# A 512-token transformer block pair on Trainium2: the memory-key norms move from the differential-attention stage into the mix-output stage, and the last retention norm moves back by a tile

## What is computed

```python
def hybrid_mixer(h, w_in, ret_norm, diff_q_norm, diff_k_norm, ..., diff_norm, w_out, lam_init):
    ...
    ro = group_norm(retention(rq, rk, rv), ret_norm)      # 4 heads of 128
    ro = jax.nn.silu(rg) * ro
    dq = rms_norm(dq, diff_q_norm)                        # 4 heads of 2 x 64
    dk = rms_norm(dk, diff_k_norm)
    do = diff_attention(dq, dk, dvv, lam)                 # softmax 0 less lam times softmax 1
    do = rms_norm(do, diff_norm) * (1.0 - lam_init)       # 4 heads of 128
    return jnp.concatenate([ro, do], axis=-1) @ w_out     # "mix_out", added to x

def memory_attention(h, mem_n, w_q, w_kv, w_o, q_norm, k_norm):
    q = rms_norm(h @ w_q, q_norm)
    k = rms_norm(mem_n @ w_k, k_norm)                     # 256 memory rows, 4 heads of 256
    ...
```

## Time and profile before

| what | value |
|---|---|
| median of three executions | 2153.44 us |
| the profiled execution's own time | 2153.9 us |
| its span in the trace | 2152.1 us |
| TensorE busy | 2098.6 us, 98% of the span |
| GpSimd busy | 1387.0 us, 64% |
| VectorE busy | 752.6 us, 35% |
| ScalarE busy | 509.4 us, 24% |
| mean granted clock of TensorE | 0.993 of full speed |

### The profile page before, as it was taken

The page is one execution under the profiler, slowest core; times in us unless marked ns, Lnnn a source line. Parts: engine busy times, 40 slices in busy tenths (PEclk is TensorE's granted clock), DMA queues, the critical chain, the costliest instruction groups (busy, mean ns, idle before and its releaser), DMA issues.

```text
span 2152.1 us, 28985 instructions
## 1 busy us (share of the span) xinstructions
PE 2098.6 (98%) x9198; PEld 1671.6 (78%) x9198; DVE 752.6 (35%) x1230; ACT 509.4 (24%) x923; POOL 1387.0 (64%) x1372
## 2 busy tenths in 40 slices
PE   7999999999999999999999999999899999999997
PEld 5878866678888888878888887877667778888885
DVE  4123345434320122352223136344765452221024
ACT  2023234331210121241111012144652322110011
POOL 5743333367776777667777779655667457777675
PEclk8999999999999999999999999999999999999998
DMA  7311111123223323222233334222222112223221
GB/s 247 114 60 40 49 50 49 50 72 97 95 98 97 98 97 107 88 91 95 97 97 98 95 98 168 88 69 74 84 88 92 56 63 93 97 97 98 97 96 61
DMA packets 55683, 193.85 MB, mean 90 GB/s; under 512 B 6303, under 2 KB 8607, under 8 KB 55236
## 3 DMA queue, kind: packets, MB, share of 16 engines
q1 hardware_dynamic: 51500, 184.05, 26.1%
q10 hardware_dynamic: 4120, 8.95, 1.3%
HBM read 190.85 MB, written 5.27 MB: 91 GB/s over the span
## 4 chain that ended last, share of the span: by engine, by line
PE 92%; DVE 4%; ACT 2%; issue 1%; DMA 0%; DVEq 0%; SPq 0%; ACTq 0%
PE acc L270 26%; PE acc L272 26%; PE acc L271 26%; PE st L316 2%; PE ob L648 1%; PE sc L633 1%; PE ob L461 1%; PE sc L474 1%; PE sc L1499 1%; PE sc L476 1%; PE acc L860 1%; PE acc L859 1%; PE tp L641 1%; PE acc L858 1%; PE st L596 1%
## 5 line engine op out<-in xcount | busy, mean ns | idle before, releaser
L1704 POOL TENSOR_TENSOR w_lo<-w_raw,w_hi 128x512 fp32r<-128x512 f32 x684 | 923.3, 1350 | 57.1
L1702 POOL TENSOR_SCALAR w_hi<-w_raw 128x512 fp32r<-128x512 f32 x684 | 466.0, 681 | 688.5 <-PE acc L272 645.4
L270 PE MATMUL acc<-h_hi,w_hi 128*128 128x512 f32 x1872 | 753.3, 402 | 13.9 <-DVE h_lo L1837 8.7
L272 PE MATMUL acc<-h_hi,w_lo 128*128 128x512 f32 x1872 | 731.4, 391 | 0.0
L271 PE MATMUL acc<-h_lo,w_hi 128*128 128x512 f32 x1872 | 730.9, 390 | 0.0
L270 PEld LDWEIGHTS acc<-h_hi,w_hi 128*128 128x128 f32 x1872 | 353.4, 189 | 102.0 <-issue 24.1
L271 PEld LDWEIGHTS acc<-h_lo,w_hi 128*128 128x128 f32 x1872 | 353.4, 189 | 82.3 <-issue 10.4
L272 PEld LDWEIGHTS acc<-h_hi,w_lo 128*128 128x128 f32 x1872 | 352.8, 188 | 74.5
L270 PE MATMUL acc<-hid_hi,w_hi 128*128 128x512 f32 x608 | 236.9, 390 | 0.0
L271 PE MATMUL acc<-hid_lo,w_hi 128*128 128x512 f32 x608 | 236.5, 389 | 0.0
L272 PE MATMUL acc<-hid_hi,w_lo 128*128 128x512 f32 x608 | 236.5, 389 | 0.0
(11 more groups left out here) (253 smaller groups left out, 1905.4 us busy)
## 6 DMA issues: line engine op xcount, KB each, us to landing
w_raw<-in_wstream SPq DMA_DIRECT2D x342, 512.0 KB, 3.5
x<-in_xT SPq DMA_DIRECT2D x4, 512.0 KB, 6.7
bias_skew<-bias_rows ACTq DMA_DIRECT2D x4, 512.0 KB, 7.6
out_y<-x SPq DMA_DIRECT2D x8, 256.0 KB, 2.2
arena<-bias_skew ACTq DMA_DIRECT2D x4, 257.5 KB, 3.6
bias_skew<-bias_rows ACTq DMA_DIRECT2D x4, 256.0 KB, 7.6
arena<-in_memT ACTq DMA_DIRECT2D x1, 1024.0 KB, 7.2
arena<-in_decay ACTq DMA_DIRECT2D x1, 1024.0 KB, 11.9
```

The source lines that it names most:

```text
L270: nc.tensor.matmul(dst, w_hi[:, slot, k, :], xh[:, k, :], start=first, stop=False)
L272: done = nc.tensor.matmul(dst, w_lo[:, slot, k, :], xh[:, k, :], start=False, stop=last)
L1702: nc.gpsimd.tensor_scalar(w_hi[:, slot, ks, :], w_raw[:, raw, ks, :], 1.0, 0.0, ALU.mult, ALU.add).then_inc(w_rounded, 1)
L1704: nc.gpsimd.tensor_tensor(w_lo[:, slot, ks, :], w_raw[:, raw, ks, :], w_hi[:, slot, ks, :].bitcast(F32), ALU.subtract).then_inc(w_split, 1)
```

## The change

The stats of the memory keys leave the attention stage. Their four squares are made at once on ACT at the start of the mix-output stage, into `pt_2`; PE runs `stat_pe` of `mk0` to `mk3` after units 2, 3, 4 and 5 of the mix output; ACT runs the stat's four steps after the squares of the same block; DVE runs L340 and L347 of `mk{n-3}` after the addition of block n, and the scaling of the keys at the end of block n, for n from 3 to 6. In the attention stage the stats now lie in tiles 4 (`dq3`), 5 (`do0`), 8 (`dk3`), 9 (`do1`), 13 (`do2`); the scaling of `do` follows its stat in the same tile on DVE, its square is made in the tile of the copy out of PSUM on ACT, and the low part stays in the head's last tile. The last retention norm (`gn3`) runs on DVE in tile 0 after the copy of the first `mem_k` unit, its ACT part in tile 0 after the exponentials, its high part in tile 1 and its low part in tile 2; since the gate in slot 31 lives longer, a probability buffer moves from slot 31 to slot 30. In the mix output ACT writes the scaled block to PSUM (`tp`), copies it to the high part from there, and writes the square to PSUM (`sc`); DVE's low part and running sum read PSUM with one SBUF operand each.

```diff
-DIFF_STAT = {2: "dq3", 3: "dk3", 4: "mk0", 5: "mk1", 6: "do0", 8: "mk2", 9: "mk3", 10: "do1", 14: "do2"}
-STATS += [DIFF_STAT[_t] for _t in sorted(DIFF_STAT)] + ["do3"]
+DIFF_STAT = {4: "dq3", 5: "do0", 8: "dk3", 9: "do1", 13: "do2"}
+STATS += [DIFF_STAT[_t] for _t in sorted(DIFF_STAT)] + ["do3"] + [f"mk{_h}" for _h in range(4)]
...
-        p_d = [[a2(28), a2(29)], [a2(32), a2(31)]]
+        p_d = [[a2(28), a2(29)], [a2(32), a2(30)]]
...
         def diff_act(act):
...
+                if tile == 0:
+                    stat_act(act, "gn3", hr[:], 128)
                 if tile in DIFF_STAT:
                     stat_of(tile)
                 if h and qt == 0:
                     o_copy(h - 1)
+                    o_sq(h - 1)
...
                 copy_pt(h, qt)
-                if tile + 1 in DIFF_STAT and DIFF_STAT[tile + 1][:2] == "mk":
-                    k_sq(int(DIFF_STAT[tile + 1][2]))
-                if h and qt == 1:
-                    o_sq(h - 1)
-                if h and qt == 3:
+                if tile == 1:
+                    ret_high_act(act, 3)
+                if h and qt == 2:
                     high(h - 1)
...
         def diff_dve(dve):
...
-                if tile == 0:
-                    ret_low_dve(dve, 3)
                 if tile < 8:
                     dve.wait_ge(w_used, 2 * (U0["mem_k"] + tile + 1))
                     nc.vector.tensor_copy(mem_k[:, tile, :], acc[tile % 2][:, 0:MEM]).then_inc(acc_read, 1)
+                if tile == 0:
+                    ret_norm_dve(dve, 3)
+                if tile == 2:
+                    ret_low_dve(dve, 3)
                 if tile in DIFF_STAT:
                     name, j = DIFF_STAT[tile], int(DIFF_STAT[tile][2])
-                    if name[:2] == "mk":
-                        k_norm(j)
-                    elif name[:2] == "do":
+                    if name[:2] == "do":
                         stat_v_dve(dve, name, 128)
+                        o_norm(j)
...
         def mix_out_pe(pe):
...
                 out1(pe, "mix_out", n, n % 2, h2_hi, h2_lo)
+                if 2 <= n < 6:
+                    h = n - 2
+                    stat_pe(pe, f"mk{h}", [pt_2[:, h, 0:MEM], pt_2[:, h, MEM:2 * MEM]], [(s("mk_sq"), h + 1)], width=MEM)

         def mix_out_act(act):
+            g, b0, s0 = GAINS["norm_mem_q_2"], blocks0("mix_out"), sums0("mix_out")
+            for h in range(4):
+                nc.scalar.activation(pt_2[:, h, :].rearrange("p (b t) -> p b t", b=2), mem_k[:, 2 * h:2 * h + 2, :],
+                                     ACT.Square).then_inc(s("mk_sq"), 1)
             for n in range(8):
-                split_act(act, "mix_out", n, n % 2, h1_hi, "norm_mem_q_2", (acc_read, G0["mix_out"] + n + 1))
+                act.wait_ge(acc_read, G0["mix_out"] + n + 1)
+                act.wait_ge(h_lo, b0 + n - 1)
+                nc.scalar.activation(tp[n % 2], x[:, n, :], ACT.Identity, scale=gain[:, g + n:g + n + 1]).then_inc(s("mo_xg"), 1)
+                act.wait_ge(s("mo_xg"), n + 1)
+                nc.scalar.copy(h1_hi[:, n, :], tp[n % 2]).then_inc(h_hi, 1)
+                act.wait_ge(h_sum, s0 + n)
+                nc.scalar.activation(sc[n % 2], x[:, n, :], ACT.Square).then_inc(h_sq, 1)
+                if 2 <= n < 6:
+                    stat_act(act, f"mk{n - 2}", hr[:, 0:MEM], 256, width=MEM)

         def mix_out_dve(dve):
...
                 nc.vector.tensor_tensor(x[:, n, :], acc[n % 2], x[:, n, :], ALU.add).then_inc(acc_read, 1)
-                split_dve(dve, "mix_out", n, n % 2, h1_hi, h1_lo, "norm_mem_q_2")
+                if 3 <= n < 7:
+                    h = n - 3
+                    stat_dve(dve, f"mk{h}", hr[:, 0:MEM], 256, MEM)
+                dve.wait_ge(h_hi, b0 + n + 1)
+                nc.vector.tensor_tensor(h1_lo[:, n, :], tp[n % 2], h1_hi[:, n, :].bitcast(F32), ALU.subtract).then_inc(h_lo, 1)
+                dve.wait_ge(h_sq, b0 + n + 1)
+                dve.wait_ge(h_sum, s0 + n + 1)
+                nc.vector.tensor_tensor(ssum[:], sc[n % 2], ssum[:], ALU.add).then_inc(h_sum, 1)
+                if 3 <= n < 7:
+                    for c in range(2):
+                        z = mem_k[:, 2 * h + c, :]
+                        nc.vector.scalar_tensor_tensor(z, z, g_col("mk", c), hr[:, 0:MEM], ALU.mult, ALU.mult).then_inc(s("mk_done"), 1)
+                    dve.wait_ge(s("mk_done"), 2 * h + 2)
+                    dve.sem_inc(hr_used, 1)
```

More of the change, by code:

```diff
@@ L1096, in ret_high_act, with ret_norm_dve @@
             nc.scalar.copy(h2_hi[:, h, :], tmp[:, 2, :]).then_inc(s("r_hi"), 1)
+        def ret_norm_dve(dve, h):
+            stat_dve(dve, f"gn{h}", hr[:], 128)
+            dve.wait_ge(s("r_xc"), h + 1)
+            nc.vector.scalar_tensor_tensor(tmp[:, 0, :], tmp[:, 1, :], g_col("ret"), hr[:], ALU.mult, ALU.mult).then_inc(s("r_y"), 1)
+            dve.wait_ge(s("r_y"), h + 1)
+            dve.sem_inc(hr_used, 1)
+            dve.wait_ge(s("r_silu"), h + 1)
+            dve.wait_ge(s("r_lo"), h)
+            nc.vector.tensor_tensor(tmp[:, 2, :], tmp[:, 0, :], a2(31), ALU.mult).then_inc(s("r_m"), 1)
         def ret_low_dve(dve, h):
@@ L1124, in retention_act @@
                 dsq(2 * h + 1)
-                stat_act(act, f"gn{h}", hr[:], 128)
                 if h < 3:
+                    stat_act(act, f"gn{h}", hr[:], 128)
                     ret_high_act(act, h)
@@ L1167, in retention_dve @@
                     dec(h + 1, 1)
[L1168 to L1181, removed]
+                    ret_norm_dve(dve, h)
                     ret_low_dve(dve, h)
+            dve.wait_ge(s("alibi_in"), 16)
+            d_scored_dve(dve, 0, 0, 0)
+            d_scored_dve(dve, 0, 0, 1)
         def mem_in_act(act):
@@ L1341, in o_sq @@
                 nc.scalar.activation(sq[:, h % 2, :], tmp[:, 0, :], ACT.Square).then_inc(s("d_osq"), 1)
[L1343 to L1350, removed]
             def stat_of(tile):
                 name = DIFF_STAT[tile]
-                if name[:2] == "mk":
-                    stat_act(act, name, hr[:, 0:MEM], 256, width=MEM)
-                else:
-                    stat_act(act, name, hr[:], 128 if name[:2] == "do" else 64)
+                stat_act(act, name, hr[:], 128 if name[:2] == "do" else 64)
             def v_copy(c):
@@ L1413, in combine @@
                 nc.vector.scalar_tensor_tensor(p0, p1, rl[:, k + 1:k + 2], p0, ALU.mult, ALU.add).then_inc(s("d_a"), 1)
[L1415 to L1421, removed]
             def o_norm(h):
@@ L1429, in o_norm, with o_low @@
                 dve.sem_inc(hr_used, 1)
+            def o_low(h):
                 dve.wait_ge(s("d_hi"), h + 1)
@@ L1454, in diff_dve @@
                 if h and qt == 3:
-                    o_norm(h - 1)
+                    o_low(h - 1)
             stat_v_dve(dve, "do3", 128)
             o_norm(3)
+            o_low(3)
         def mix_out_pe(pe):
@@ L1468, in mix_out_pe @@
                 out1(pe, "mix_out", n, n % 2, h2_hi, h2_lo)
+                if 2 <= n < 6:
+                    h = n - 2
+                    stat_pe(pe, f"mk{h}", [pt_2[:, h, 0:MEM], pt_2[:, h, MEM:2 * MEM]], [(s("mk_sq"), h + 1)], width=MEM)
         def mix_out_act(act):
+            g, b0, s0 = GAINS["norm_mem_q_2"], blocks0("mix_out"), sums0("mix_out")
+            for h in range(4):
+                nc.scalar.activation(pt_2[:, h, :].rearrange("p (b t) -> p b t", b=2), mem_k[:, 2 * h:2 * h + 2, :],
+                                     ACT.Square).then_inc(s("mk_sq"), 1)
             for n in range(8):
-                split_act(act, "mix_out", n, n % 2, h1_hi, "norm_mem_q_2", (acc_read, G0["mix_out"] + n + 1))
+                act.wait_ge(acc_read, G0["mix_out"] + n + 1)
[7 more added lines that the diff above has]
+                    stat_act(act, f"mk{n - 2}", hr[:, 0:MEM], 256, width=MEM)
         def mix_out_dve(dve):
+            b0, s0 = blocks0("mix_out"), sums0("mix_out")
             nc.vector.memset(ssum[:], 0.0).then_inc(h_sum, 1)
```

4 lines of the change are left out of this document (removed).

## The result

The changed kernel takes 2161.38 us (median of six executions, 2159.56 to 2163.04) against 2153.84 (2151.01 to 2156.46): slower, ratio 1.003, 95% interval 1.0018 to 1.0043. The prediction said 2154.0 with a range to 2158.0. The profiled execution took 2159.96 us.

The account below looks back on a forecast made before the run. TensorE was taken as the bound, busy 2098.6 of 2152.1 us. Attention stage -3.4 and mix-output stalls +3.9 made +0.5 us, 2153.9 on the median, stated as 2154.0; range 2149.5 to 2158.0.

Parts of the forecast that it names:

- Mix output: Mix-output stage: TensorE stalls three times behind units 3 to 5 on the stat bank, 1.3 us each, adding 3.9 us.
- PSUM scratch: Mix output: two late VectorE operations per block shorten by about 0.4 us each, 6.5 us in all, none of it TensorE's.
- The attention stage without the key norms: Attention stage: four stats of 0.85 us leave, 3.4 us in all, and waits fall from 10.9 to 7.45 us.
- Turns 6 and 10: Attention stage: TensorE's transposes in tiles 6 and 10 wait 1.2 us each behind a norm of `do` on VectorE.
- the squares: Attention stage, tiles 5, 9 and 13: stats of `do` wait 0.35 us each for ScalarE's square, 1.05 in all.
- turn 14: Attention stage: TensorE's transposes in tile 14, which had no wait from this sequence, now wait 0.7 us.
- The last retention norm: Start of the attention stage: moving the norm shifts TensorE's wait of 1.46 us one tile later, at 1.5 us.
- The norm ends at 1511.9: VectorE, tile 0: the moved norm begins at about 1508.7, with the 3.15 us read from its old place.
- The wait before turn 1: Attention stage: TensorE waits 1.5 us before the transposes of tile 1, and not before those of tile 0.
- The rival on the slower side: Mix output: ScalarE's steps wait for the shared `hr`, stalls grow to 2.5 us each; 2157.6 to 2159.6 us; chance 13%.

Follow-up runs that it names:

- e2: Changed kernel with VectorE's read of the stat bank moved ahead of the next block's addition, key scaling right behind that addition: 2156.43 us, ratio 1.0012.
- e4: Changed kernel with the mix output's scaled block and squares kept in SBUF as before: 2161.45 us.
- e1: Changed kernel with the last retention norm back in its old place, before tile 0: 2156.36 us, ratio 1.0006 to the kernel before.
- e8: e5 with the stats that stay in the attention stage, their squares, norms and high parts in their old tiles: 2148.96 us, ratio 0.9974.
- e3: Changed kernel with the late retention norm's intermediate results in a free PSUM bank: 2158.44 us, ratio 1.0024.
- e10: Kernel before the change with only the last retention norm moved to its later place: 2159.59 us, ratio 1.0025.
- e5: Changed kernel with e1 and e2 together: 2151.97 us, ratio 0.9994.
- e7: e6 with the last retention norm spread, one VectorE instruction in each of tiles 0 to 3: 2148.53 us, ratio 0.9973.
- e9: e7's spread retention norm, `do` stats in their old tiles, `dq3` and `dk3` in the new ones: 2151.4 us, ratio 0.9987.
- e6: e5 with the norms of `do` one tile later on VectorE, high and low part in the head's last tile: 2151.34 us, ratio 0.9983.
- e11: e9 with the low part of the retention norm moved from tile 7 to tile 5: 2146.6 us, ratio 0.997.

## Why the prediction was wrong

- **Mix output: right.** The one bank `st`, L340 behind the addition, three stalls, all as written; 1.38 us each for 1.3, and 0.91 for 0.85 per moved stat. e2 shows it by removing it.
- **PSUM scratch: right.** VectorE was spared 5.1 us for the 6.5 forecast, TensorE none (e4).
- **The attention stage without the key norms: right in mechanism and size.** With the retention norm left in place it gave 6.55 us (e1), forecast 3.4 + 3.4 = 6.8. Turns 6 and 10 waited 1.68 and 1.78 for 1.2, the squares 0.47 each for 0.35, turn 14 0.50 for 0.7, turn 15 0.38 for none. That it came so close is in part luck. PE's idle time in the stage fell from 99.13 - 88.93 (busy) = 10.2 us to 92.58 - 84.74 = 7.8 in e1, so the waits gave 2.4 and not 3.4; the other 4.2 us are 1.05 for each stat taken away, for 0.85. That the new placement itself costs 2.7 us (e8) was in these waits, but I had set them down as kept and not as caused.
- **The last retention norm: this step failed.** "The norm ends at 1511.9" took its 3.15 us from rows where GpSimd stood idle for the first 1.9 of them, and moved them to a place where it never does. Measured: 5.17 us, 2.02 more, and a combine of 0.89 instead of 0.48. The wait before turn 1 was 4.05 and not 1.5; e3 brings it back to 1.61 by taking away one SBUF operand. I had the spread of the two-operand instructions in the earlier trace rows, and used it for the mix output, where it did not matter, and not for the norm, where it did.
- **The clock had no term.** Two stretches at the lower level begin in or behind waits in the changed kernel. With the norm in its late place PE's path is 99.25 - 92.58 = 6.67 us longer, of which the wait explains 2.6 and the clock 4.0. Of these 4.0, the 2.5 behind turn 1 come back when the norm alone is moved (2.4 in e10); for the 1.6 behind turn 10 the cause stays open. The changed kernel, e2 and e4 all have that fall and e1 and e5 do not, but the wait before the turn is the same in all five (1.75 to 1.79 us), and how the norm's move would reach that far no run shows. Without the norm's move the kernel takes 2156.36 us (e1), inside the range.
- **The rival on the slower side** (the hand-over of `hr`) did not happen: the stalls stayed at 1.11 in the records, all three alike.

## What to carry to other kernels

A duration read from a row belongs to its neighbourhood. Before a block of VectorE work with two SBUF operands is moved, look at GpSimd's timeline at both places, and price it with the stretched rows if GpSimd is busy at the new one. A norm that must stand in a queue before something TensorE waits for costs its undivided length; spread over tiles, one instruction each, it cost 0.35 us before one turn (e7). Each of these instructions still needs a tile with room: its low part in tile 7 cost e9 1.86 us. And reading a shared bank ahead of the next wait took away three stalls without removing work (e2).

## What the runs showed of the hardware

The spread between executions of one kernel goes with the granted clock. In the first series the kernel before ran 29 times: 6 executions with a mean clock of 0.994 took 2151.0 us on average, 14 at 0.993 took 2153.8, 5 at 0.992 took 2155.5 and 4 at 0.990 took 2159.2. So a profile, being one execution, can hold a fall of the clock or miss it, and a stage that is clean in one profile need not be so in every execution.

The length of a single wait did not decide it. The clock fell in or behind waits of 4.05 us (changed, e10), 1.86 (e9), 1.78 (changed) and 1.61 (e3), and behind two of 0.96 and 0.68 in a row (e6), but not behind 2.00 (e11), nor behind 1.70 and 1.77 (e5), although e3's 1.70 and 1.76 at the same turns were each followed by a fall. In the changed kernel it fell at 1512.9, 2.6 us into the wait; in e3 at 1513.0, when TensorE had been busy again for 1.8 us. What sets it was not found; no run was made for it alone. Where it fell, the granted clock was the lower of its two levels, the 1.2 GHz one, for 3.4 us (e3, e6, e9, the second fall in the changed kernel) or, with the 4.05 us waits, for 6.8 us, of which 1.5 to 1.8 passed in the wait; matmuls of 512 columns stood 0.43 us apart instead of 0.23. What it cost depends on what TensorE waited for next: 2.5 and 1.6 us in the changed kernel, nothing in e9, where the next transposes had to wait for VectorE in any case.
